# Weight-stationary chunks of the ReLU stages and gated mixers: one 512-column product for the high half of the weight, the halves added by VectorE

## What is computed

```
h = rms_norm(x, norm1_g)
z = h @ w_in                     # 1024 -> 8704, 17 chunks of 512 columns
zq, zf, zi, zg, zatt, za, zb = split(z, (512, 512, 512, 512, 4608, 1024, 1024))
q = silu(zq); f from sigmoid(zf); k = 1 - f; v = zi       # gated recurrence, 4 heads of 128
o_hg = rms_norm(hgrn2_chunked(q, log f, k, v)) * sigmoid(zg)
o_att = three groups of dilated window attention over zatt (rotated q, k)
y = sigmoid(za) * (o_hg @ w_branch_a) + sigmoid(zb) * (o_att @ w_branch_b)
x = x + y @ w_out
h2 = rms_norm(x, norm2_g)
x = x + square(relu(h2 @ w_up)) @ w_down      # 1024 -> 4096 -> 1024
```

## Time and profile before

| what | value |
|---|---|
| median of 3 executions | 1913.79 us (1913.39 to 1916.04) |
| the profiled execution: span from first to last instruction | 1913.3 us |
| mean granted clock of TensorE | 0.995 |
| TensorE busy | 1884.5 us, 98% |
| VectorE busy | 1259.2 us, 66% |
| ScalarE busy | 968.4 us, 51% |
| moved by DMA | 342.52 MB, mean 179 GB/s |

### The profile page before, as it was taken

The page is one execution under the profiler, slowest core; times in us unless marked ns, Lnnn a source line. Parts: engine busy times, 40 slices in busy tenths (PEclk is TensorE's granted clock), DMA queues, the critical chain, the costliest instruction groups (busy, mean ns, idle before and its releaser), DMA issues.

```text
span 1913.3 us, 26911 instructions
## 1 busy us (share of the span) xinstructions
PE 1884.5 (98%) x10465; PEld 1638.4 (86%) x10465; DVE 1259.2 (66%) x1598; ACT 968.4 (51%) x1242; POOL 35.8 (2%) x67
## 2 busy tenths in 40 slices
PE   9999999999999999999999999999999999999998
PEld 7788877888888888788879998889988998889987
DVE  4466777455646677845576887676556787776654
ACT  5454564454445456455446445455544645554543
POOL 1010100000000000000000000000000000000000
PEclk9999999999999999999999999999999999999999
DMA  9567535665666664576545554465565554455662
GB/s 319 176 191 222 194 112 188 194 180 179 212 192 183 181 185 140 163 216 186 185 145 187 177 182 131 134 203 182 187 190 184 182 185 153 125 177 178 185 193 82
DMA packets 173580, 342.52 MB, mean 179 GB/s; under 512 B 10976, under 2 KB 11152, under 8 KB 173344
## 3 DMA queue, kind: packets, MB, share of 16 engines
q1 hardware_dynamic: 169360, 327.26, 54.7%
q0 software_dynamic: 4112, 13.77, 2.1%
HBM read 338.36 MB, written 1.05 MB: 177 GB/s over the span
## 4 chain that ended last, share of the span: by engine, by line
PE 91%; DVE 6%; ACT 2%; issue 1%; DMA 0%; DVEq 0%; SPq 0%; ACTq 0%
PE stream L2203 18%; PE stream L2205 18%; PE stream L2204 18%; PE stream L2370 7%; PE stream L2371 7%; PE stream L2372 7%; PE aux L2250 3%; PE aux L2611 1%; PE stream L2241 1%; DVE wlo L1242 1%; PE stream L2309 1%; PE stream L2232 1%; PE stream L2233 1%; PE stream L2311 1%; PE stream L2310 1%
## 5 line engine op out<-in xcount | busy, mean ns | idle before, releaser
L1242 DVE TENSOR_TENSOR wlo<-raw,whi 128x1024 fp32r<-128x1024 f32 x584 | 707.7, 1223 | 535.6 <-ACT whi L716 532.6
L716 ACT ACTIVATE whi<-raw 128x1024 fp32r<-128x1024 f32 x584 | 612.3, 1057 | 619.2 <-PE stream L2205 435.4
L2203 PE MATMUL stream<-whi,xhi 128*128 128x512 f32 x944 | 373.3, 395 | 1.7 <-DVE wlo L1242 1.7
L2205 PE MATMUL stream<-whi,xlo 128*128 128x512 f32 x944 | 368.6, 390 | 0.0
L2204 PE MATMUL stream<-wlo,xhi 128*128 128x512 f32 x944 | 368.2, 390 | 0.0
L2370 PE MATMUL stream<-xhi,whi 128*128 128x256 f32 x1184 | 337.4, 285 | 0.0
L2371 PE MATMUL stream<-xlo,whi 128*128 128x256 f32 x1184 | 335.4, 283 | 0.0
L2372 PE MATMUL stream<-xhi,wlo 128*128 128x256 f32 x1184 | 335.3, 283 | 0.0
L2203 PE MATMUL stream<-whi,hhi 128*128 128x512 f32 x672 | 263.3, 392 | 0.0
L2205 PE MATMUL stream<-whi,hlo 128*128 128x512 f32 x672 | 261.6, 389 | 0.0
L2204 PE MATMUL stream<-wlo,hhi 128*128 128x512 f32 x672 | 261.5, 389 | 0.0
(11 more groups left out here) (334 smaller groups left out, 1757.6 us busy)
## 6 DMA issues: line engine op xcount, KB each, us to landing
raw<-ffn_w_gu SPq DMA_DIRECT2D x176, 512.0 KB, 4.4
raw<-w_in SPq DMA_DIRECT2D x136, 512.0 KB, 4.7
raw<-ffn_w_down SPq DMA_DIRECT2D x88, 512.0 KB, 3.7
raw<-w_up SPq DMA_DIRECT2D x64, 512.0 KB, 4.0
raw<-w_down SPq DMA_DIRECT2D x64, 512.0 KB, 3.6
raw<-c_w_in SPq DMA_DIRECT2D x24, 512.0 KB, 4.0
raw<-ab_w_in SPq DMA_DIRECT2D x20, 512.0 KB, 5.3
raw<-w_out SPq DMA_DIRECT2D x16, 512.0 KB, 3.6
```

Of the source, the lines that this page charges most:

```text
L716: act.activation(split_slots(lin, at, j)[0], raw[:, b % RAW], ACT.Copy).then_inc(hi_ready, 1)
L1242: dve.tensor_tensor(lo, raw[:, b % RAW], hi.bitcast(F32), ALU.subtract).then_inc(lo_ready, 1)
L2203: pe.matmul(bank[tt][:], hi, wh, start=kt == 0, stop=False)
L2205: mm = pe.matmul(bank[tt][:], lo, wh, start=False, stop=kt == last)
```

## The change

Thirty chunks go from the columns form to a form called `paired`: chunks 1, 2 and 4 to 9 of `w_in` in both mixers and chunks 1 to 7 of `w_up` in both ReLU stages. `xhi` and `xlo` become two halves of one tensor `x_split`. For a weight tile the high part is multiplied with x's high and low parts in one matmul of 512 columns, which fills one PSUM bank: its first half holds whi x xhi, its second whi x xlo. The low part's product wlo x xhi (256 columns) is added to the second half. So the four output tiles of a chunk fill all four `stream` banks, tiles 0 and 1 in the chunk's own pair and 2 and 3 in the other pair. The last two blocks are walked tile by tile, in the order 2, 3, 0, 1, and both are counted as used only with the last tile.

ScalarE copies the first half of a bank (`copy_halves`), VectorE adds the second (`add_halves`): three pieces for each chunk, tiles 2 and 3 together, tile 0, tile 1. Both stand behind the splits of blocks 0 and 1 of the next chunk, and ahead of those of blocks 2 and 3. Relu, Silu and the sigmoids, which were part of the eviction, are now done from SBUF: Relu as a maximum within the square on VectorE, Silu and the two sigmoids (over whole tiles) as passes of their own on ScalarE, and `forget` waits for the latter (`forgets_made`). In the ReLU stage `h_hi` and `h_lo` of the chunk before move ahead of the copy and the add.

```diff
-                    return ACT.Tanh if gate(c) else ACT.Silu if c == 2 else ACT.Copy
+                    return ACT.Tanh if gate(c) else ACT.Copy
...
                     if c == 1:
-                        at = At(1)
-                        act.wait_ge(block_used, into.done(at))
-                        for i in range(2):
-                            bank = stream[into.banks(at) + i]
-                            act.activation(columns_of(decayed[0], 0)(i), bank[:], ACT.Sigmoid)
-                            act.activation(columns_of(hk, 0)(i), bank[:], ACT.Sigmoid, scale=-1.0).then_inc(evicted, 1)
+                        act.wait_ge(evicted, 2 * (into.c0 + 1) + 2)
+                        act.activation(hk[:], decayed[0][:], ACT.Sigmoid, scale=-1.0)
+                        act.activation(decayed[0][:], decayed[0][:], ACT.Sigmoid).then_inc(forgets_made, 1)
                     if c == 2:
+                        act.wait_ge(evicted, 2 * (into.c0 + 2) + 2)
+                        act.activation(hq[:], hq[:], ACT.Silu)
...
+            def copy_halves(lin, at, dst):
+                n = lin.paired_before(at)
+                for i, (to, first, _) in enumerate(pair_halves(lin, at, dst)):
+                    if i < 2:
+                        act.wait_ge(tiles_full, 2 * n + i + 1)
+                    else:
+                        act.wait_ge(block_used, lin.done(at))
+                    act.activation(to, first, ACT.Copy).then_inc(tiles_copied, 1)
...
+            def add_halves(lin, at, dst):
+                n = lin.paired_before(at)
+                for i, (to, _, second) in enumerate(pair_halves(lin, at, dst)):
+                    dve.wait_ge(tiles_copied, 3 * n + i + 1)
+                    a = dve.tensor_tensor(to, second, to, ALU.add)
+                    if i != 1:
+                        a.then_inc(evicted, 1)
...
                         if j < to.kb:
                             rest(to, at, j, j + 1)
+                        if j == 1 and c in lin.paired:
+                            add_halves(lin, At(c), place(c))
...
+        def freed(lin, at):
+            if at.like:
+                before_paired = at.like - 1 in lin.paired
+            else:
+                before_paired = lin is not lins[0] and preceding(lin).n - 1 in preceding(lin).paired
+            return 2 * (lin.chunk(at) - 1) + before_paired
...
+            def paired(lin, at, hook=None):
+                own, other, last = lin.banks(at), 2 - lin.banks(at), SPLIT * BK - 1
+                banks = [stream[i] for i in (own, own + 1, other, other + 1)]
+                pe.wait_ge(evicted, freed(lin, at))
+                def products(j, m):
+                    wh, wl = (w[:, :, m * P:(m + 1) * P] for w in split_slots(lin, at, j))
+                    for k in range(BK):
+                        kt = j * BK + k
+                        both, to = x_split[:, :, kt], banks[m].rearrange("p (a t) -> p a t", a=2)
+                        if kt < last:
+                            pe.matmul(to, wh[:, k], both, start=kt == 0, stop=False)
+                        mm = pe.matmul(to[:, 1], wl[:, k], xhi[:, kt], start=False, stop=False)
+                        if kt == last:
+                            mm = pe.matmul(to, wh[:, k], both, start=False, stop=True)
+                    return mm
+                for j in range(SPLIT - 2):
+                    b, turn = lin.block(at, j)
+                    if hook:
+                        hook(j)
+                    pe.wait_ge(lo_ready, split_count(b, turn))
+                    for m in range(4):
+                        if (j, m) == (0, 2):
+                            pe.wait_ge(evicted, 2 * lin.chunk(at))
+                        mm = products(j, m)
+                    mm.then_inc(block_used, 1)
+                for m in (2, 3, 0, 1):
+                    if hook and m in (2, 0):
+                        hook(SPLIT - 2 if m else SPLIT - 1)
+                    for j in (SPLIT - 2, SPLIT - 1):
+                        if m == 2:
+                            b, turn = lin.block(at, j)
+                            pe.wait_ge(lo_ready, split_count(b, turn))
+                        mm = products(j, m)
+                        if m == 1:
+                            mm.then_inc(block_used, 1)
+                    if m in (3, 0):
+                        mm.then_inc(tiles_full, 1)
...
                 def body(at):
-                    split(up, At(at.like + 1, at.turn))
+                    after = At(at.like + 1, at.turn)
+                    split(up, after, 0, 2)
+                    h_hi(At(at.like - 1, at.turn))
                     act.wait_ge(h_lo_ready, l0 + at.c - 2)
-                    relu(at)
-                    h_hi(At(at.like - 1, at.turn))
+                    halves(at)
+                    split(up, after, 2)
...
-                    dve.tensor_tensor(part, part, part, ALU.mult).then_inc(h_made, 1)
+                    dve.scalar_tensor_tensor(part, part, 0.0, part, ALU.max, ALU.mult).then_inc(h_made, 1)
```

More of the change, by code:

```diff
@@ L253, with __init__ @@
 class Linear:
-    def __init__(self, w, k, n, order=(), walk=None):
-        self.order, self.walk = order, walk
+    def __init__(self, w, k, n, order=(), walk=None, paired=()):
+        self.order, self.walk, self.paired = order, walk, paired
         self.w, self.kb, self.n = w, k // (P * BK), n // CH
-        self.b0 = self.c0 = 0
+        self.b0 = self.c0 = self.paired0 = 0
         self.early = None
@@ L281, in banks, with paired_before @@
         return 2 * ((self.c0 + at.like) % 2)
+    def paired_before(self, at):
+        like = sum(c < at.like for c in self.paired)
+        return self.paired0 + like + 2 * at.turn
     def done(self, at):
@@ L429, in program @@
         branch_b = sb("branch_b", [P, TT, D], at=42 * KB)
-        stream = [ctx.enter_context(nc.psum_tensor(f"stream{i}", [P, CH], F32)) for i in range(4)]
+        streams = ctx.enter_context(nc.psum_tensor("stream", [P, 4, CH], F32))
+        stream = [streams[:, i] for i in range(4)]
         aux = [ctx.enter_context(nc.psum_tensor(f"aux{i}", [P, CH], F32)) for i in range(AUX)]
@@ L438, in program @@
         ident = cst("ident")
+        tiles_from = lambda dst, first: lambda a, b: dst[:, first + a:first + b, :]
+        relu_tiles = lambda at: lambda a, b: relu_part[at.like % 2][:].rearrange("p a (b t) -> p (a b) t", b=2)[:, a:b]
         raw_in = [sem(f"raw_in{i}") for i in range(RAW)]
@@ L503, in program @@
         bound_exp = sem("bound_exp")
+        forgets_made = sem("forgets_made")
         f_ready = sem("f_ready")
@@ L513, in program @@
                 lin.c0 = before.c0 + before.n
+                lin.paired0 = before.paired0 + len(before.paired)
         lins = LINS(stages)
@@ L572, in preceding, with pair_halves @@
             return lins[lins.index(lin) - 1]
+        def freed(lin, at):
[4 more added lines that the diff above has]
+            return 2 * (lin.chunk(at) - 1) + before_paired
+        def pair_halves(lin, at, dst):
+            own, other = lin.banks(at), 2 - lin.banks(at)
+            parts = ((dst(2, 4), streams[:, other:other + 2]), (dst(0, 1), streams[:, own:own + 1]),
+                     (dst(1, 2), streams[:, own + 1:own + 2]))
+            return [(to, bank[:, :, 0:S], bank[:, :, S:CH]) for to, bank in parts]
         block = ctx.enter_context(nc.Block())
@@ L744, in layer @@
                             split(to, at, j, j + 1)
-                    if place(c) is not None:
+                        if j == 1 and c in lin.paired:
+                            copy_halves(lin, At(c), place(c))
+                    if place(c) is not None and c not in lin.paired:
                         evict(lin, At(c), place(c), func(c), scale(c))
@@ L1170, in ffn2, with halves @@
                 a0 = seen.aux
-                def relu(at):
-                    evict(up, at, lambda i: relu_part[at.like % 2][:, i, :], ACT.Relu)
+                def halves(at):
+                    copy_halves(up, at, relu_tiles(at))
                 def h_hi(at):
@@ L1876, in forget @@
                         step(dve.tensor_tensor(rest_of, rest_of, high, ALU.mult))
-                    dve.wait_ge(evicted, 2 * (into.c0 + 1) + 2)
+                    dve.wait_ge(forgets_made, st.layer + 1)
                     for h in range(HEADS_G):
@@ L2067, in beside, with place @@
                     return within
-                layer(into, use, beside(into, -48))
+                def place(c):
+                    if c < 4:
+                        return tiles_from(decayed[0] if c == 1 else hq, 0)
+                    return tiles_from(aq if c < 7 else ak, 4 * ((c - 4) % 3))
+                layer(into, use, beside(into, -48), place)
                 def gated_a(c):
@@ L2345, in columns @@
                 if not isinstance(at.turn, int) or lin.chunk(at) >= 2:
-                    pe.wait_ge(evicted, 2 * (lin.chunk(at) - 1))
+                    pe.wait_ge(evicted, freed(lin, at))
```

(10 more changed lines are left out.)

57 lines of the change are left out of this document (34 added, 23 removed).

## The result

The changed kernel takes 1922.77 us, the median of 4 runs (1921.61 to 1924.35). The kernel before, run beside it, takes 1913.74 (1913.39 to 1916.04, 4 runs). The ratio is 1.0047, with a 95% interval of 1.0035 to 1.0059. The change makes the kernel slower by 9.0 us. (Four later executions, of e6, e7 and the kernel before, took from 8% to four times longer than the rest and are left out of ranges and ratios.)

A forecast was written before the change was run, and what follows sets the result against it. The prediction took TensorE, busy 98% of the span, as the bound; -12.2 + 5.8 + 4.8 + 4.0 + 2.8 + 1.6 = +6.8 us on 1913.3, plus 0.5, gave 1920.6, forecast 1920.5 us, range 1909 to 1927 (its own 1917 to 1924).

The forecast's parts named there:

- Chunk 1 waits for the banks: Chunk 1 of all four stages: TensorE waits for ScalarE's eviction of chunk 0, 1.45 us each, 5.8 us lost.
- Chunk 4 waits for the banks: Chunk 4 of both mixers: TensorE waits for ScalarE's eviction of chunk 3, 2.4 us each, 4.8 us lost.
- Chunk 3 waits for VectorE: Chunk 3's start in both mixers: VectorE adds chunk 2's tiles late, behind forget steps and splits; 2.0 us each, 4.0 lost.
- The gain on TensorE: Thirty paired chunks: a unit falls from 360 to 347 ns, a chunk by 0.405 us, 12.2 us gained.
- The prediction's lower bound from the step from 256 to 512 columns: Alternative TensorE reading: 0.23 us for the 512-column matmul after the step, 350 ns a unit, gain 9.4 us.
- Saturated periods and the lag into the attention part: Mixers: VectorE becomes the bound in chunks 5 to 9, 2.8 us lost; its lag reaches the attention part, 1.6 us lost.
- Paired chunks don't wait for each other: Borders between paired chunks: banks released after 1.12 us against 1.39 needed, so no stall, 0.27 us of cover.
- the rival's price: Slower rival (20%): hand-overs between paired chunks miss their cover by 0.2 us, 22 of them costing 4.4 us.
- ReLU stages shorter by 1.5 us each: Expected sign in the trace: each ReLU stage shorter by 1.5 us, while mixers grow by about 5.
- the smaller VectorE part: Rival (25%): VectorE hides the forget chain, saturated periods and lag, 8.4 us, leaving only the bank waits; 1912.2 us.
- The faster mix: Rival (10%): 256-column weight loads lie wholly beneath the 512 columns before, 320 ns a unit; 1903 us.
- The fall of the clock in the new gaps: Part of the slower rival (20%): the clock falls in TensorE's new gaps; 3.4 us at 1.2 GHz would cost 1.7 us.

The follow-up runs named there:

- e6: Changed kernel with VectorE's forget part one chunk later (behind chunk 2) and ScalarE's logarithm of it inside chunk 3; 1922.94 us, ratio 1.0042 to the kernel before.
- e7: Changed kernel with e3, e5 and e6 together and the second half's decay exponentials behind chunk 4's copies; 1909.26 us, ratio 0.9975 to the kernel before.
- e3: Changed kernel with ScalarE evicting chunks 0 and 3 earlier, and a tiny Tanh loading the table ahead of chunk 3's eviction; 1914.72 us, ratio 1.0006 to the kernel before.
- e4: Kernel before with only a TensorE wait added in chunks 1 and 4, for the previous chunk's full eviction; 1927.76 us, ratio 1.0074 to the kernel before.
- e2: Changed kernel with each block's two 512-column products grouped ahead of the two 256-column ones (last block reversed); 1922.51 us, ratio 1.0039 to the kernel before.
- e5: Changed kernel with the last k-tile keeping the order 512 then 256, so no 256-column products are neighbours; 1920.08 us, ratio 1.0038 to the kernel before.
- e1: Changed kernel with x's high and low part of each k-tile side by side in SBUF; 1922.29 us, ratio 1.0047 to the kernel before.

## Why the prediction was right

Forecast 1920.5 us, measured 1922.77: inside its own narrow range (1917 to 1924), 2.3 us low. The places, the causes of the waits and the sign were right, and the two bank waits came out to the tenth. The other terms were too high, the gain and the losses alike, so that their errors cancel in part: that the time came within 2.3 us is partly luck. Point by point, with chunk lengths from start to start in the two traces:

- **Chunk 1 waits for the banks** (forecast 1.45 x 4 = 5.8). Measured 1.43 x 4 = 5.7. The release came 2.83 us after the chunk's start, forecast 2.84. e3 takes it away, e4 makes it alone.
- **Chunk 4 waits for the banks** (2.4 x 2 = 4.8). Measured 2.36 x 2 = 4.7, released 3.77 us after the start, forecast 3.78.
- **Chunk 3 waits for VectorE** (2.0 x 2 = 4.0). Measured 1.67 + 1.74 = 3.4. VectorE's own timeline in the changed kernel, as the prediction had put it step by step:

```profile
1021.88 0.41 DVE L1933 TENSOR_SCALAR decayed<-decayed,bound 128x256 f32<-128x256 f32 x1 [1.90 <-ACT decayed L1136]
...
1025.97 2.36 DVE L1284 TENSOR_TENSOR wlo<-raw,whi 128x1024 fp32r<-128x1024 f32 x2
1028.25 1.35 DVE L1295 TENSOR_TENSOR hq<-stream,hq 128x512 f32<-128x512 f32 x3
```

  Forget part, two splits, three adds, in that order, where before the splits of chunk 3 ended the sequence. e6 turns the order and the wait is gone.
- **The gain on TensorE** (30 x 0.405 = 12.2) was the term that was mis-sized most. Six chunks of a ReLU stage fell from 69.20 to 67.61 us, 0.265 each; chunk 1 there, without its wait, only from 11.51 to 11.40, and the eight chunks of a mixer by 1.9 together. That is 1.7 us in a ReLU stage and 1.9 in a mixer, 7.1 in all. The prediction's lower bound from the step from 256 to 512 columns, 9.4 us at 350 ns a unit, was the better reading of the earlier trace rows, and still too high. By 960 dropped matmuls, one gave back 7.4 ns (8.3 in the six chunks), not 13. The Trainium skill's fixed cost of about 2.5 ns for a matmul (TensorE: Matmul & The Clock Gate, Part 1) does not agree here either: the estimate by it is 2.4 us in all, where 7.1 were measured.
- **Saturated periods and the lag into the attention part** (2.8 + 1.6 = 4.4). Mixers grew by 4.46 + 4.81 = 9.3 us. Taking 5.7/2 + 4.7 + 3.4 for the waits and returning 3.7 of gain leaves 2.0. VectorE did become the bound, as said, but at 13.23 us a period and not 13.35, and TensorE's need is 11.2 + 1.79 = 13.0 and not 12.9; the pair differ by 0.2 and not by 0.46. The part behind chunk 9 grew by 0.55 and 0.80 us (165.66 to 166.21 and 166.46), near the 0.8 forecast for each, but only 0.2 of it is the named wait of the attention part's transposes for ScalarE's scaled weights.
- **Paired chunks don't wait for each other**: right. In the first mixer chunk 2 follows chunk 1 at 1016.05; chunk 1's last copy ran from 1016.25 and its last add ended at 1017.09, 1.04 us into chunk 2, forecast 1.12 and cover 1.39. There are 24 such borders, not 22, which matters only to the rival's price. The six chunks above show TensorE busy for 67.61 of 67.61 us.
- **ReLU stages shorter by 1.5 us each**: measured 0.3, all of it by the smaller gain.

The measured terms, -7.1 + 5.7 + 4.7 + 3.4 + 2.0, make the +8.7 us by which the stages grew; the medians grew by 9.0. Against the forecast of +6.8, a gain too high by 5.1 stood beside losses too high by 3.2. Of the rivals, the smaller VectorE part (1912.2) was half true of the saturated periods and false of chunk 3. The faster mix (1903) was false: even at the faster pace a unit took 346 to 347 ns in the mean. The fall of the clock in the new gaps, which the prediction left unsettled, did not happen in the changed kernel's profiled execution, but did in those of e2, e4 and e6 behind the 2.5 us gap, for 1.7 us each time; that it is a part of the difference between 8.7 and 9.0 is not shown.

Still open: why a unit has two paces, 346 to 347 and about 353 ns in the mean, and what starts the slow one in the third unit of chunks 1 and 4; what decides whether the clock falls behind a given gap; and whether e7's last wait, at chunk 6, can be ordered away too, which no run tried.

## What to carry to other kernels

Work moved off a saturated engine pays only where the engine that takes it has slack in that stage: with the big hand-over waits mended, the same change lost 0.7 and 1.3 us in the mixers, where VectorE was idle a tenth of the period, and won 2.7 to 2.9 in a ReLU stage, where it was idle two fifths. When a chunk comes to need all buffers instead of half, look first at its borders with chunks of the old kind: six such borders cost more here than thirty chunks won. And price a dropped instruction by a run of the new mix where one can be had; the fixed part read from long runs of one width, 13 ns, stood against 7 to 8 that a dropped product gave back.

## What was not expected of the hardware

- The same alternation of a 512- and a 256-column product, with weights loaded before each, runs at two paces. Four units in the first ReLU stage of e5 took 1.39 us (starts at 1319.83 and 1321.22), in the changed kernel 1.41 (1319.66 and 1321.07). In e5 the pace holds over whole chunks. In the changed kernel it turned slow behind two neighbouring 256-column products, and in chunks 1 and 4 it was slow from the third unit on, ahead of any gap. What starts it is open.
- A gap of 2.5 us between dense matmuls was followed by a fall of the granted clock in e4 and e6 (both mixers) and in e2 (once), and not in the changed kernel, e1 and e5, in one profiled execution of each. e4 and the changed kernel show mean clocks of 0.79 and 1.00 over the same 8 us with 5.8 us of TensorE's work in each. It costs 1.7 us when it happens, two thirds of the gap itself.
